# Group B's weighing of the values: two query tiles in turn on two column tiles of TensorE

## The reference

```python
def row_fn(args):                       # one grid row of 64 queries
    r, r0, q_row = args                 # r0 = clip(r - kh//2, 0, rows - kh), kh = min(8, rows)
    k_strip = lax.dynamic_slice_in_dim(kg, r0, kh, axis=1)
    v_strip = lax.dynamic_slice_in_dim(vg, r0, kh, axis=1)
    bias = rpb_c[:, dr_idx].transpose(0, 2, 1, 3)
    sc = jnp.einsum('bqhd,bikhd->bhqik', q_row, k_strip) * scale + bias[None]
    sc = jnp.where(col_ok[None, None, :, None, :], sc, -jnp.inf)
    p = jax.nn.softmax(sc.reshape(b, h, GRID_W, kh * GRID_W), axis=-1)
    p = p.reshape(b, h, GRID_W, kh, GRID_W)
    return jnp.einsum('bhqik,bikhd->bqhd', p, v_strip)
```

## Time and profile before

| | us |
|---|---|
| median of 3 runs (lowest, highest) | 2346.83 (2346.11, 2348.16) |
| the profiled execution's own time | 2346.19 |
| its span, first to last instruction | 2344.4 |
| TensorE busy (matmul) | 2244.3 |
| VectorE busy | 1621.0 |
| ScalarE busy | 804.2 |
| GpSimd busy | 291.1 |
| mean granted TensorE clock | 0.982 of 2.4 GHz |

### The profile page before, as it was taken

How to read it: one execution, slowest core, us unless ns; L and a number is a source line. 1 busy time by engine, 2 the same in 40 slices (tenths; PEclk the granted TensorE clock), 3 DMA queues, 4 the chain that set the end, 5 groups by cost and what they waited for, 6 DMA issues and landing times.

```text
span 2344.4 us, 30421 instructions
## 1 busy us (share of the span) xinstructions
PE 2244.3 (96%) x11036; PEld 1831.4 (78%) x11036; DVE 1621.0 (69%) x2144; ACT 804.2 (34%) x1297; POOL 291.1 (12%) x183
## 2 busy tenths in 40 slices
PE   7999999999899999998999999999999999987996
PEld 5777887777787778877888888888888888865884
DVE  7777428888866666656777677776777767765545
ACT  6222117777655562132222112221222212144223
POOL 5101001000000013420000000000000000024101
PEclk9999999999999999999999999999999999998997
DMA  5223346110255503101101011010100101010102
GB/s 167 104 85 117 146 137 142 27 27 14 49 111 110 110 1 144 36 18 36 36 27 36 27 36 35 28 36 27 36 30 33 36 27 36 27 55 18 45 28 108
DMA packets 51021, 137.48 MB, mean 59 GB/s; under 512 B 20240, under 2 KB 20752, under 8 KB 50960
## 3 DMA queue, kind: packets, MB, share of 16 engines
q1 hardware_dynamic: 50096, 135.55, 19.5%
q10 hardware_dynamic: 864, 1.13, 0.1%
HBM read 105.99 MB, written 30.67 MB: 58 GB/s over the span
## 4 chain that ended last, share of the span: by engine, by line
PE 85%; DVE 9%; ACT 2%; issue 1%; DMA 1%; POOL 0%; SPq 0%; DVEq 0%; ACTq 0%; POOLq 0%
PE ps L297 23%; PE ps L299 23%; PE ps L298 23%; PE ps L1008 4%; PE ps L984 3%; PE ps L1014 3%; DVE nmax L1167 2%; PE ps L973 2%; PE ps L974 2%; DVE PTL L1188 1%; DVE NL L1787 1%; PE ps L992 1%; PE ps L495 1%; PE ps L490 1%; DVE NL L1468 1%
## 5 line engine op out<-in xcount | busy, mean ns | idle before, releaser
L297 PE MATMUL ps<-NH,WH 128*128 128x512 f32 x1896 | 759.6, 401 | 35.1 <-DVE WL L293 10.6
L298 PE MATMUL ps<-NL,WH 128*128 128x512 f32 x1896 | 745.3, 393 | 0.0
L299 PE MATMUL ps<-NH,WL 128*128 128x512 f32 x1896 | 744.8, 393 | 0.0
L297 PEld LDWEIGHTS ps<-NH,WH 128*128 128x128 f32 x1896 | 360.5, 190 | 123.6 <-issue 25.3
L298 PEld LDWEIGHTS ps<-NL,WH 128*128 128x128 f32 x1896 | 360.5, 190 | 80.1 <-issue 6.0
L299 PEld LDWEIGHTS ps<-NH,WL 128*128 128x128 f32 x1896 | 360.2, 190 | 76.4
L1719 DVE TENSOR_TENSOR H<-H,ps 128x512 f32<-128x512 f32 x480 | 305.5, 682 | 104.1 <-PE ps L299 104.1
L274 POOL TENSOR_TENSOR raw<-raw,gains 128x1024 f32<-128x1024 f32 x76 | 152.3, 2008 | 1342.8 <-DMA raw<-in_w 1342.8
L289 ACT ACTIVATE WH<-raw 128x1024 fp32r<-128x1024 f32 x102 | 107.8, 1057 | 574.1 <-PE ps L299 544.7
L297 PE MATMUL ps<-MH,WH 128*128 128x512 f32 x504 | 197.1, 391 | 6.8 <-DVE H L1794 6.8
L299 PE MATMUL ps<-MH,WL 128*128 128x512 f32 x504 | 196.3, 390 | 0.0
(11 more groups left out here) (172 smaller groups left out, 2793.4 us busy)
## 6 DMA issues: line engine op xcount, KB each, us to landing
raw<-in_w SPq DMA_DIRECT2D x102, 512.0 KB, 3.3
xst<-in_xT SPq DMA_DIRECT2D x24, 256.0 KB, 3.4
H<-in_xT SPq DMA_DIRECT2D x8, 768.0 KB, 9.6
out_yT<-H SPq DMA_DIRECT2D x24, 256.0 KB, 2.1
qkh<-oqh SPq DMA_DIRECT2D x5, 768.0 KB, 3.3
qkl<-oql SPq DMA_DIRECT2D x5, 768.0 KB, 4.9
qkh<-obh SPq DMA_DIRECT2D x5, 768.0 KB, 3.5
qkl<-obl SPq DMA_DIRECT2D x5, 768.0 KB, 5.9
```

The lines of the kernel that those rows point to most:

```text
L297: nc.tensor.matmul(out, wh, xh, start=first, stop=False)
L298: nc.tensor.matmul(out, wh, xl, start=False, stop=False)
L299: return nc.tensor.matmul(out, wl, xh, start=False, stop=last)
```

## The change

For group B, `weigh_both` takes the place of the two calls of `weigh`. It goes over the key blocks of both tiles at once: block 0 of the first, block 0 of the second, block 1 of the first, and so on. The first tile's result goes to PSUM partitions 0 to 63, the second's to 64 to 127 of the same bank and the same 128 columns; four tiles now take 256 columns of 128 partitions. The number of matmuls, their operands and their sizes are those of before. The waits for both tiles' probabilities stand ahead of the first matmul. The read-out copies each half of the partitions with an instruction of its own into the places of `H` that belong to it; the first raises `o_copy` and the second `o_sum`, and the multiply waits for both.

```diff
-                if kind == "B":
-                    for kb, kn, n in todo:
-                        mm = nc.tensor.matmul(ps[0:DH, PVBANK, at:at + queries], VF[s][0:kn, k0 // P + kb, 0:DH],
-                                              PF[0:kn, (m // 2) % 2, n, c0:c0 + queries],
-                                              start=kb == 0, stop=kb == todo[-1][0])
-                    return mm
+            def weigh_both(p, b, m):
+
+                s = b // 3
+                for bank in range(2):
+                    pe.wait_ge(t_free[bank], fills("B", p, ("T", m + 1)) + T_FREE)
+                at_least(pe, o_sum, p * 6 + b)
+                windows = [window("B", x) for x in (m, m + 1)]
+                for blocks in zip(*(places(w) for _, w, _, _ in windows), strict=True):
+                    for half, (kb, kn, n) in enumerate(blocks):
+                        mm = nc.tensor.matmul(ps[cols(half, DH), PVBANK, cols((m // 2) % 2, P)],
+                                              VF[s][0:kn, windows[half][0] // P + kb, 0:DH],
+                                              PF[0:kn, (m // 2) % 2, n, cols(half, P)],
+                                              start=kb == 0, stop=kb == len(places(windows[half][1])) - 1)
+                return mm
...
                 if kind == "B" and m % 2 == 0:
-                    weigh(kind, p, (m - 2) // 4, m - 2, P)
-                    mm = weigh(kind, p, (m - 2) // 4, m - 1, P)
+                    mm = weigh_both(p, (m - 2) // 4, m - 2)
...
                     dst = H[rows, bass.ds(p, 1), cols(g)].rearrange("p a n -> p (a n)")
-                    nc.vector.tensor_copy(dst, ps[0:DH, PVBANK, :]).then_inc(o_sum, 1)
+                    by_half = dst.rearrange("p (t h q) -> p t h q", h=2, q=P)
+                    for half, done in enumerate((o_copy, o_sum)):
+                        v = ps[cols(half, DH), PVBANK, 0:2 * P].rearrange("p (t q) -> p t q", q=P)
+                        nc.vector.tensor_copy(by_half[:, :, half, :], v).then_inc(done, 1)
+                    dve.wait_ge(o_copy, p * 6 + b + 1)
                     dve.wait_ge(o_sum, p * 6 + b + 1)
                     nc.vector.tensor_tensor(dst, dst, ps[rows, RBANK, :], ALU.mult).then_inc(o_done, 1)
```

## The result

The changed kernel took 2325.43 us (median of 4 runs, 2323.08 to 2329.14) against 2346.86 before: a ratio of 0.991, with a 95% interval of 0.9892 to 0.9927. That is 21.4 us less, where 26.8 were forecast (2320 us); 2310 to 2348 was the range. The profiled execution has a span of 2321.3 us, 23.1 less than before; it is the fastest of the four.

A forecast was written before the change was run, and what follows sets the result against it. TensorE was taken to bound Group B, with VectorE idle for 82 of 239 us. Terms -4.5 -38.4 +2.9 +9.2 +0.8 +2.7 = -27.3 from 2346.2 gave 2318.9, forecast 2320 us; range 2310 to 2348.

The forecast's parts named there:

- (a): Group B's weighing calls of 20 passes: one change of tile shape inside the call, not three; saves 4.5 us.
- (b): Two column tiles in turn in Group B's weighing: saves 38.4 us with full overlap, 20.4 with exposed loads, 0 with none.
- the likeliest case: Group B's weighing: passes on different tiles run at once, and so do their loads; 38.4 us saved, chance 38%.
- 1a starts with 0b: The second tile's first pass starts with the first tile's second, at 0.109 us; calls of 16 passes save 0.763 us.
- The sign of full overlap: Group B's pieces of 16 passes last 1.2 us if passes and loads on the two tiles overlap fully.
- "middle" case: Rival: matmuls overlap, but a load starts only once the matmul ahead has started; calls save 20.4 us, 2330 us, 25%.
- no overlap: Rival: the second column tile is only another place for the result, passes stay 0.108 us apart; 2345 us, 22%.
- slower by the alternation: Rival: each of 352 alternations waits for the matmul in flight (2363 us) or drains the array (2395 us); 15%.
- (c): VectorE's read-out in two copies takes 0.12 us more, on the path in all 24 read-outs: + 2.9 us.
- (d): TensorE's waits in `weigh_both`, for bank fills and `o_sum`, add nothing: 0.
- (e): What Group B's saving runs into: VectorE's bias tables give back 9.2, 0.8 and 2.7 us at the upper end.
- the two signs by which it named itself wrong: Passes keep their step of 0.108 us, or VectorE's waits take far more than the 15.6 us given for them.

The follow-up runs named there:

- the seam mended: Changed kernel with table load issued earlier and read-out shared between ScalarE and VectorE, plus one VectorE wait for GpSimd's sum in the next stage: 2306.78 us, ratio 0.9829.
- the table first: Changed kernel with the next bias table's load issued ahead of the wait for the scores and the other loads: 2314.43 us, ratio 0.9866.
- the filler: Changed kernel with unused matmuls of 256 columns added ahead of turns in steps 5 and 6 of each Group B pair: 2320.78 us, ratio 0.9889.

## Why the prediction was right, and where it was off

(a) Changes of tile shape: right. The gaps ahead of the loads fell from 91 recorded to 63 (64 forecast), and the run with turns on one tile has calls of 2.47 us, as worked out. That its time came out at the very 4.5 us is in part luck, with an interval from 1.6 to 7.5; in its trace Group B is 2.2 us shorter.

(b) Overlap: the direction and the likeliest case were right, the size too small. Forecast: 38.4 us for (b) and 42.9 with (a). Measured in calls: 49.1 for both. The step that failed is "1a starts with 0b": the second tile's first pass starts with the first's first (one step of 0.109 us less in each of 48 calls is 5.2 of the 6.2 us that were missing). I had taken it that a pass waits its turn behind both passes of the matmul in front; the run without turns shows that it goes ahead of three queued ones. (The sign of full overlap that was named, 1.2 us for 16 passes, was itself rounded up from 1.13 by the forecast's own sum.) The bound of the "middle" case, that a load starts only once the matmul ahead has started, fell with it. The rivals "no overlap" and "slower by the alternation" are out: an alternation costs nothing that shows in 1.02 us for 16 passes. The rule of the Trainium skill (TensorE: Matmul & The Clock Gate, Part 3) on weight loads and row groups, by which the time would have been 2363 us, doesn't hold here: loads for both column tiles ran beside matmuls of the same rows in these 1.02 us.

(c) The copies: 48 of 0.421 us, as forecast, and a pair of them takes 0.86 to 0.88 us, 0.18 to 0.20 more than the one copy; I had 0.12. The 80 ns of overlap that I deducted aren't there. That they lie on the path, by themselves, the run with only the two copies could not show. That VectorE's queue in front of the turns' bank is part of what remains is shown by the runs with a shared read-out: with half the copying on ScalarE and the seam mended, 2314.4 became 2306.8, 7.6 us, for 24 x 0.43 = 10.3 us taken off that queue. In the traces 4.4 of it are in Group B.

(d) TensorE's waits at 0: nothing in the trace speaks against it.

(e) What was given back: 15.6 us with the copies were forecast, 27.7 measured. The place was right, and 11.0 of them are the bias table's, which the table first gave back; forecast were 9.2 + 0.8 there. But its make-up was wrong: no term stood for the clock. I had read the 1.00 of Group B as a given, though the longest wait of a turn for VectorE was 1.0 us there; with waits of 2 us it fell three times, and the filler shows about 4.7 us of it or more. The rest is VectorE: 16.2 us more of waiting for its bank in the list, 10 of it still there with the table first, where I had expected 2.7 us in three cycles only and slack everywhere else. The average over a cycle (6.5 us of VectorE in 8) hid that its work comes in a clump: read-out, multiply, copy, one after the other, just when TensorE has nothing but a short score and a turn to do. The chain shows the second copy, the multiply, the bank's copy and then the turn:

```profile
660.51 0.44 DVE H L1214
...
661.04 0.07 DVE H L1217
...
661.64 0.42 DVE PF L1192
...
662.11 0.44 PE ps L984 x2
```

Of the 27.7, 11.0 and 7.6 were recovered by runs; 9.1 stay unassigned between the remaining waits (10.4 us for VectorE's bank in the fastest version) and a spread of 6 us among the changed kernel's runs. That what a run recovers is what the change gave back is itself argued: a copy moved off VectorE also shortens waits that were there before. The spread goes with the clock: the four runs have 2323.08, 2324.48, 2326.38 and 2329.14 us at a mean granted clock of 0.978, 0.977, 0.976 and 0.975.

The forecast thus came within 5.4 us by luck, as two errors stood against each other: 6.2 us too little gain in the calls and 12.1 us too little given back. Of the two signs by which it named itself wrong, the second, waits that take far more than 15.6 us, came in the main: 27.7 us, of which some 5 are the clock's.

## What to carry to other kernels

A matmul whose stationary operand is only 64 columns wide leaves half of the array free; give a second, independent sum the other column tile and put the two in turn (one or two blocks at a time), and nothing is lost by the turns: 16 passes in 1.02 us for 1.89. Then look at once for what the long matmuls were hiding: a transfer that is issued late, an engine's clump of work in front of a bank, and the clock, which fell here, most times, where TensorE had come to wait for 2 us. In a forecast, an engine's average load over a cycle is no measure of slack; go through the cycle instruction by instruction with the call shortened.

## What the runs showed of the hardware

- Two plain f32 matmuls on the column tiles of one 128x64 shape run at the full pace of each: 8 + 8 passes take 1.02 us, seven steps of 0.109 and one record of 0.27, and two begin within 25 ns.
- TensorE starts a pass for the free column tile ahead of passes queued in front of it for the busy one: three of them in the run without turns, and no more; the second tile waited while four stood in front.
- A stretch in which TensorE was busy for 3.08 of 6 us was followed by ten at 1.2 GHz, in which it was busy all the time and did the work more slowly. 88 useless matmuls that prevented this saved 4.7 us; at the head of the next stage ten of them made the stretch to L316 2.3 us shorter, which the kernel's time did not show.
- A GpSimd sum that takes 1.27 us took 11.64 beside gapless subtractions of VectorE with two SBUF inputs in one version, and 2.64 when VectorE left a gap. In the kernel before and others it took 1.4 to 1.7 beside the same subtractions, one of which took 1.78 us for 0.68.
